# Gated FFN up projections as seven block products per weight tile pair

## The reference

```python
def swiglu(x, w_in, w_out):
    gate, up = jnp.split(x @ w_in, 2, axis=-1)
    return (jax.nn.silu(gate) * up) @ w_out

for l in range(DEPTH):       # DEPTH = 2, D_MODEL = 1024, D_FF = 2816, SEQ = 512, float32
    x = x + 0.5 * rms_norm(swiglu(rms_norm(x, ln_ffn1_pre[l]), w_ffn1_in[l], w_ffn1_out[l]), ln_ffn1_post[l])
    mix = token_mixing(rms_norm(x, ln_mix_pre[l]), ...)
    x = x + rms_norm(mix, ln_mix_post[l])
    x = x + 0.5 * rms_norm(swiglu(rms_norm(x, ln_ffn2_pre[l]), w_ffn2_in[l], w_ffn2_out[l]), ln_ffn2_post[l])
    gate = jax.nn.sigmoid(rms_norm(x, ln_ple_pre[l]) @ w_ple_gate[l])
    x = x + rms_norm(gate * (p[l] @ w_ple_proj[l]), ln_ple_post[l])
```

## Time and profile before

| | |
|---|---|
| time, median of 3 runs | 2898.39 us (2896.41 to 2900.55) |
| span of the profiled execution | 2896.7 us |
| PE busy | 2846.7 us, 98% |
| PE weight loads busy | 2402.4 us, 83% |
| DVE busy | 1379.2 us, 48% |
| ACT busy | 1141.2 us, 39% |
| POOL busy | 15.7 us, 1% |
| granted TensorE clock, mean | 0.997 |
| 512-column matmuls of L214 | 6048, mean 390 ns each from start to end |
| 256-column matmuls of L214 | 1536, mean 286 ns |

### The profile page before, as it was taken

The page is one execution under the profiler, slowest core; times in us unless marked ns, Lnnn a source line. Parts: engine busy times, 40 slices in busy tenths (PEclk is TensorE's granted clock), DMA queues, the critical chain, the costliest instruction groups (busy, mean ns, idle before and its releaser), DMA issues. The chain is left out here.

```text
span 2896.7 us, 41108 instructions
## 1 busy us (share of the span) xinstructions
PE 2846.7 (98%) x17248; PEld 2402.4 (83%) x17248; DVE 1379.2 (48%) x1923; ACT 1141.2 (39%) x1655; POOL 15.7 (1%) x29
## 2 busy tenths in 40 slices
PE   8999999999999999999999999999999999999998
PEld 7888888878888888888888877888888888888887
DVE  3334355676333355333336667333346258756541
ACT  3223244554232245222235555223236357544430
POOL 0000000000000000000000000000000000000000
PEclk9999999999999999999999999999999999999999
DMA  4233412103223431223412103122332111222331
GB/s 152 96 101 126 142 39 66 39 3 117 87 95 109 138 117 52 92 97 107 149 49 79 53 4 110 61 100 95 132 122 95 59 49 33 102 73 96 101 124 51
DMA packets 71415, 254.32 MB, mean 88 GB/s; under 512 B 8056, under 2 KB 9080, under 8 KB 71232
## 3 DMA queue, kind: packets, MB, share of 16 engines
q1 hardware_dynamic: 71232, 251.70, 25.9%
HBM read 249.57 MB, written 2.10 MB: 87 GB/s over the span
## 5 line engine op out<-in xcount | busy, mean ns | idle before, releaser
L214 PE MATMUL ps<-h_hi,w_space 128*128 128x512 f32 (+1 forms) x5056 | 1445.8, 370 | 3.0 <-DVE h_lo L312 3.0
L214 PEld LDWEIGHTS ps<-h_hi,w_space 128*128 128x128 f32 x5056 | 919.1, 189 | 163.8 <-DVE h_lo L312 3.8
L202 DVE TENSOR_TENSOR w_space<-w_raw,w_space 128x1024 fp32r<-128x1024 f32 x440 | 533.5, 1223 | 1015.7 <-ACT w_space L195 1015.6
L214 PE MATMUL ps<-h_lo,w_space 128*128 128x512 f32 (+1 forms) x2528 | 930.9, 368 | 0.0
L195 ACT CAST w_space<-w_raw 128x1024 fp32r<-128x1024 f32 x440 | 455.8, 1048 | 898.9 <-PE ps L214 551.1
L224 PE MATMUL ps<-w_space 128*128 128x512 f32 x3216 | 737.3, 390 | 1.3 <-PEq L91 0.8
L224 PEld LDWEIGHTS ps<-w_space 128*128 128x128 f32 x3216 | 602.0, 188 | 125.9 <-issue 1.2
L214 PEld LDWEIGHTS ps<-h_lo,w_space 128*128 128x128 f32 x2528 | 477.9, 189 | 77.5 <-issue 0.5
L607 ACT CAST w_space<-act_p 128x512 fp32r<-128x512 f32 x88 | 54.7, 621 | 186.1 <-DVE act_p L619 186.1
L622 DVE TENSOR_TENSOR w_space<-act_p,w_space 128x512 fp32r<-128x512 f32 x88 | 60.9, 692 | 60.5 <-ACT w_space L607 60.5
L619 DVE TENSOR_TENSOR act_p<-act_s,ps 128x512 f32<-128x512 f32 x88 | 59.9, 680 | 54.9 <-PE ps L214 54.9
(11 more groups left out here) (412 smaller groups left out, 2195.5 us busy)
## 6 DMA issues: line engine op xcount, KB each, us to landing
w_raw<-in_w_ffn_in SPq DMA_DIRECT2D x176, 512.0 KB, 3.4
w_raw<-in_w_ffn_out SPq DMA_DIRECT2D x88, 512.0 KB, 3.5
w_raw<-in_w_in SPq DMA_DIRECT2D x64, 512.0 KB, 3.4
w_raw<-in_w_up SPq DMA_DIRECT2D x44, 512.0 KB, 3.4
w_raw<-in_w_out SPq DMA_DIRECT2D x24, 512.0 KB, 4.0
w_raw<-in_w_down SPq DMA_DIRECT2D x22, 512.0 KB, 3.5
w_raw<-in_w_ple_gate SPq DMA_DIRECT2D x16, 512.0 KB, 3.5
gain_pre<-in_gains_pre SPq DMA_DIRECT2D x10, 512.0 KB, 4.8
```

The lines of the kernel that those rows point to most:

```text
L202: nc.vector.tensor_tensor(self.lo(n), self.raw[:, n % SLOTS, :], self.hi(n).bitcast(F32), ALU.subtract).then_inc(self.lo_ready, 1)
L214: m = nc.tensor.matmul(c.ps[:, bank, t], part[:, cols], moving[:, k, t], start=(k == 0 and i == 0), stop=(k == KD - 1 and i == 2))
```

## The change

A gate tile G and an up tile U over the halves of the contraction are the 2 x 2 blocks a11, a12 (of G) and a21, a22 (of U). h over the same halves and over the two halves of the tokens is b11, b12, b21, b22. The four blocks of the result are made from seven products instead of eight (Winograd's form), for pairs 3 to 21. Pairs 0 to 2 (`PLAIN = 3`) stay as they were.

The sums are s1 = a21 + a22, s2 = s1 - a11 ("early sums", `sums_early`), s3 = a11 - a21, s4 = a12 - s2 ("late sums"), t1 = b12 - b11, t2 = b22 - t1, t3 = b22 - b12, t4 = b21 - t2. s are made for every pair on DVE, t once an FFN; POOL first adds h_hi and h_lo again to whole values. Each operand of a product is split in hi and lo. The partial results are added in PSUM: ACT copies between halves of banks ("seeded"), and to SBUF ("kept", "carried"), and DVE adds them back ("c", "d").

```diff
-            ffn1.append(Ffn(c, turn, a["w_ffn1_in"][l], a["w_ffn1_out"][l], AFTER_PLE if l else FRESH, **after_ple))
+            ffn1.append(SevenFfn(c, turn, a["w_ffn1_in"][l], a["w_ffn1_out"][l], AFTER_PLE if l else FRESH, SPARE, **after_ple))
...
+    def tensor_product(self, pe, nc, q, name):
+        c = self.c
+        x_name, t_name, half = {"m1": ("a11", "b11", 0), "m5": ("s1", "t1", 1), "m6": ("s2", "t2", 0), "m2": ("a12", "b21", 0),
+                                "m7": ("s3", "t3", 0), "m3": ("s4", "b22", 1), "m4": ("a22", "t4", 0)}[name]
...
+        for k in range(HALF_K):
+            cols = slice(k * P, (k + 1) * P)
+            for i, (part, moving) in enumerate(((x_hi, t_hi), (x_hi, t_lo), (x_lo, t_hi))):
+                m = nc.tensor.matmul(out, part[:, cols], moving[:, k, :], start=(name == "m1" and k == 0 and i == 0),
+                                     stop=(k == HALF_K - 1 and i == 2), skip_group_check=(name != "m1"))
+        m.then_inc(c.seven_done, 1)
```

PE's order of the products, with what each waits for:

```diff
+        for q in range(PLAIN, KF):
+            if q > PLAIN:
+                pe.wait_ge(c.silu_ready, self.f0 + q - 3)
+            self.wait_rested(pe, "x", q, 0)
+            self.tensor_product(pe, nc, q, "m1")
+            self.wait_rested(pe, "x", q, 1)
+            self.tensor_product(pe, nc, q, "m5")
+            if q > PLAIN:
+                self.wait_rested(pe, "x", q - 1, 3)
+                self.wait_rested(pe, "d", q - 1)
+                self.tensor_product(pe, nc, q - 1, "m4")
+            self.wait_split(pe, "seeded", q)
+            self.tensor_product(pe, nc, q, "m6")
+            self.wait_split(pe, "kept", q)
+            self.tensor_product(pe, nc, q, "m2")
+            self.wait_split(pe, "carried", q)
+            self.wait_rested(pe, "x", q, 2)
+            self.tensor_product(pe, nc, q, "m7")
+            self.wait_rested(pe, "c", q)
+            self.tensor_product(pe, nc, q, "m3")
```

Operand part 0 is the gate unit (a11, a12), 1 the early sums, 2 the late sums, 3 the half unit a22. ACT's loop; t3's conversion and the wait for its lo stand ahead of it:

```diff
+        self.silu(act, nc, 2)
+        act.wait_ge(W.done, self.u0 + 2 * PLAIN)
+        self.t_hi(act, nc, "t3")
+        self.wait_rested(act, "t3")
+        for q in range(PLAIN, KF):
+            bank, other = self.bank(2 * q), self.bank(2 * q + 1)
+            if q > PLAIN:
+                self.silu(act, nc, q - 1)
+            self.part_hi(act, nc, q, 2)
+            if q < LAST:
+                self.part_hi(act, nc, q + 1, 0)
...
+            act.wait_ge(c.seven_done, self.done_no(q, "m5"))
+            if q > PLAIN:
+                act.wait_ge(c.product, self.f0 + q - 3)
+            nc.scalar.copy(c.ps[:, other, 0:HALF_T], c.ps[:, bank, 0:HALF_T]).then_inc(c.seven_split, 1)
+            if q >= PLAIN + 2:
+                self.wait_rested(act, "d", q - 2)
+            nc.scalar.copy(c.p[:, 0, (q % 2) * HALF_T:(q % 2 + 1) * HALF_T], c.ps[:, bank, HALF_T:S]).then_inc(c.seven_split, 1)
+            self.part_hi(act, nc, q, 3)
+            if q < LAST:
+                self.part_hi(act, nc, q + 1, 1)
...
+            act.wait_ge(c.seven_done, self.done_no(q, "m6"))
+            if q > PLAIN:
+                self.wait_rested(act, "c", q - 1)
+            nc.scalar.copy(c.p[:, 1, 0:HALF_T], c.ps[:, other, 0:HALF_T]).then_inc(c.seven_split, 1)
```

The acts are no longer split when they are made. They stay whole in the slots (`cells`), and each is split in the down phase into one of four places:

```diff
+    def act_hi(self, act, nc, k):
+        c = self.c
+        act.wait_ge(c.product, self.f0 + k + 1)
+        if k < 4:
+            act.wait_ge(c.seven_done, self.done_no(LAST, ("m5", "m6")[k // 2]))
+        else:
+            act.wait_ge(c.W.done, self.down.d0 + k - 3)
+        nc.scalar.copy(self.act_parts(k)[0], self.cell(k)).then_inc(c.act_hi, 1)
...
+    def scalar_down(self, act, nc):
+        for k in range(4, KF):
+            self.act_hi(act, nc, k)
+            self.c.W.hi_to(act, nc, self.down.d0 + k + 1)
```

`vector_down` does the same with the lo parts. The rows of w_out go through five slots in turn (`ROW_SLOTS`), so row k's conversion waits for row k-5. In the blocks these calls stand ahead of the conversions for the next phase, and SP loads all rows before it loads gains and masks (the masks still wait for `act_ready` of all 22 acts):

```diff
-                c.W.load_to(sp, ffn.down.d0 + SLOTS)
+                c.W.load_to(sp, ffn.down.d0 + KF)
+                ffn.wait_extra(sp)
                 proj.turn.load(sp)
                 attention.load(sp, ffn)
                 c.W.load_to(sp, proj.u0 + 12)
...
                 ffn.scalar(act, nc)
-                c.W.hi_to(act, nc, ffn.down.d0 + SLOTS)
                 start.scalar_tables(act, nc)
+                ffn.scalar_down(act, nc)
                 c.W.hi_to(act, nc, ffn.end() + EARLY)
                 turn_scalar(act, nc, proj.turn, ffn.down)
```

More of the change, by code:

```diff
@@ L153, with __init__ @@
 class Unit:
-    def __init__(self, n, slot, after, src):
-        self.n, self.slot, self.after, self.src = n, slot, after, src
+    def __init__(self, n, slot, after, load):
+        self.n, self.slot, self.after, self.load = n, slot, after, load
+class Load:
+    def __init__(self, src, freed):
+        self.src, self.freed = src, freed
 class Weights:
     def __init__(self, c, raw, sem):
-        self.c, self.raw, self.units, self.held = c, raw, [], {}
+        self.c, self.raw, self.units, self.loads, self.held = c, raw, [], [], {}
         self.raw_ready = [sem(f"w_raw_ready{s}") for s in range(SLOTS)]
@@ L170, in add, with add_raw @@
         n = len(self.units)
-        self.units.append(Unit(n, slot, self.held.get(slot), src))
-        self.held[slot] = n
-        return n
+        self.units.append(Unit(n, slot, self.held.get(slot), len(self.loads)))
+        self.loads.append(Load(src, (self.lo_ready, n + 1)))
+        self.held[slot] = (self.done, n + 1)
+        return n
+    def add_raw(self, src, freed):
+        self.loads.append(Load(src, freed))
+        return len(self.loads) - 1
     def hi(self, n):
@@ L179, in lo, with raw_of, wait_loaded @@
         return self.c.space[:, self.units[n].slot, 1, :]
+    def raw_of(self, i):
+        return self.raw[:, i % SLOTS, :]
+    def wait_loaded(self, eng, i):
+        eng.wait_ge(self.raw_ready[i % SLOTS], 16 * (i // SLOTS + 1))
     def load_to(self, sp, end):
[L182 to L186, removed]
+        last = self.units[end - 1].load + 1
+        while self.loaded < last:
+            i = self.loaded
+            if i >= SLOTS:
+                freed, count = self.loads[i - SLOTS].freed
+                sp.wait_ge(freed, count)
+            sp.dma_start(self.raw_of(i), self.loads[i].src).then_inc(self.raw_ready[i % SLOTS], 16)
             self.loaded += 1
@@ L191, in hi_to @@
             n = self.split
[L192 to L195, removed]
+            unit = self.units[n]
+            self.wait_loaded(act, unit.load)
+            if unit.after is not None:
+                freed, count = unit.after
+                act.wait_ge(freed, count)
+            nc.scalar.copy(self.hi(n), self.raw_of(unit.load)).then_inc(self.hi_ready, 1)
             self.split += 1
@@ L213, in products_up @@
         for i, (part, moving) in enumerate(((W.hi(n), c.h_hi), (W.hi(n), c.h_lo), (W.lo(n), c.h_hi))):
-            m = nc.tensor.matmul(c.ps[:, bank, t], part[:, cols], moving[:, k, t], start=(k == 0 and i == 0),
-                                 stop=(k == KD - 1 and i == 2))
+            m = nc.tensor.matmul(c.ps[:, bank, t], part[:, cols], moving[:, k, t], start=(opens and k == 0 and i == 0),
+                                 stop=(k == KD - 1 and i == 2), skip_group_check=not opens)
     return m
@@ L543, in wait_free @@
         if self.free[k] is not None:
-            eng.wait_ge(self.c.W.done, self.free[k] + 1)
+            freed, count = self.free[k]
+            eng.wait_ge(freed, count)
     def release(self, d0):
         for k in range(KF):
-            self.c.W.held[k // 2] = d0 + k
+            self.c.W.held[k // 2] = (self.c.W.done, d0 + k + 1)
 class Ffn(Up):
@@ L825, in __init__ @@
         for k in range(KD):
-            c.W.held[OPERANDS_AT + k // 2] = self.down.d0 + k
+            c.W.held[OPERANDS_AT + k // 2] = (c.W.done, self.down.d0 + k + 1)
     def place(self, w_out):
         self.early = EARLY_ROWS
-        self.c.W.held[MIX_OUT_SLOTS[4]] = len(self.c.W.units)
+        self.c.W.held[MIX_OUT_SLOTS[4]] = (self.c.W.done, len(self.c.W.units) + 1)
         self.down = Down(self.c, [w_out[k] for k in range(KD)], MIX_OUT_SLOTS)
```

349 lines of the change are left out of this document (337 added, 12 removed).

## The result

| | before | after |
|---|---|---|
| time, median | 2899.58 us (2896.41 to 2904.49) | 2903.26 us (2898.53 to 2910.01) |
| ratio to before, 95% interval | | 1.0013 [1.0007, 1.0019] |
| span of the profiled execution | 2896.7 us | 2900.6 us |
| granted TensorE clock, mean | 0.997 | 0.989 |

A forecast was written before the change was run, and what follows sets the result against it. The prediction took TensorE (PE), busy 2846.7 of 2896.7 us, as the bound. Its terms, -65.4 (products) + 8 (first pairs) + 36 (tails) + 6.4 (clock) = -15 us, gave 2883.4 us, range 2843 to 2912.

The forecast's parts named there:

- the tails: Ends of four FFNs: splitting acts there delays the norm before tile 0's transposes, 36 us together, bounds 10 to 46.
- Part 1, the rate: Pairs 3 to 21: 256-column matmuls start every 119.3 ns, saving 0.86 us a pair, 65.4 us over 76 pairs.
- Part 2, the walk: Seven-product loop: ACT and DVE keep up with PE, smallest slack 0.7 us, so it costs nothing.
- POOL additions ... hidden: Before the first changed pair: POOL's additions end 20 us before the products, so they cost nothing.
- The first changed pair: ACT's conversions ahead of "seeded" make m6 wait: 2.0 us, 8 us in four FFNs, bounds 0 to 12.
- Part 3, projection tails: FFN ends before projection: ACT's order and weights behind window masks stall tile 0's transposes 11.4 us, 11.1 more, twice.
- Part 3, PLE tails: FFN ends before PLE: act 21, row 21 and seven units precede the norm; stall 7.3 us, 7.0 more, twice.
- The clock: Behind the four tail stalls: PE runs at half rate for a while, 1.6 us each, 6.4 us, at least 0.
- A: Rival: tails are hidden and only the first changed pairs lose, -57 us, 2841 us; chance 0.22.
- B: Rival: ACT and DVE pace the seven-product loop, PE stopping 1 us a pair, +76, 2959 us; chance 0.11.
- C: Rival: waits at seven product boundaries a pair break up weight loads, 53 us, kernel at 2936; chance 0.05.

The follow-up runs named there:

- e9: The changed kernel with both late sums made twice in each of the 76 pairs, adding DVE work: 2902.93 us, ratio 1.0010.
- e1: The changed kernel with all four POOL additions waiting until h is whole: 2898.68 us, ratio 0.9994.
- e2: The changed kernel with copies seeded and kept ahead of the late-sum and next-gate conversions in the first changed pair: 2898.88 us, ratio 0.9998.
- e3: The changed kernel with SP loading the first three projection units ahead of the window masks: 2894.86 us, ratio 0.9983.
- e8: The kernel before the change, with ten useless ACT copies of 1024 columns ahead of the norm in the four tails: 2941.11 us, ratio 1.0141.
- e4: e3, with ACT and DVE converting only two next-phase units ahead of the norm, the others between its steps: 2862.68 us, ratio 0.9867.
- e7: The changed kernel with 34 zero-weight filler matmuls of 512 columns ahead of tile 0's transposes in the tails: 2899.99 us, ratio 0.9999.
- e10: The changed kernel with e1, e2 and e4, carried and add c earlier in first changed pairs, one lo earlier in PLE tails: 2849.65 us, ratio 0.9827.

## Why the prediction was wrong

Most mechanisms were read rightly, and the sum was not: -65 and +50 are terms that nearly cancel. The sum came out 18.7 us too low. The rate is 5.9 of it (4.6 by starts alone), the tails 4.4, the half clock behind them 3.2, the half clock behind small gaps 3.1 and POOL's additions 3.7; the last two stood at nothing. All five err in one direction.

- **Part 1, the rate,** is the largest term that was mis-sized. 119.3 ns was read over 15 starts of the earlier trace rows, where one hundredth of a microsecond in the printed starts is 0.7 ns a matmul. It is 120.0, and over 6384 matmuls that is 4.5 us. The saving was 59.5 to 60.8 us, below even the lower bound of 63.5. Both stretches that the prediction used are of some 20 matmuls. The trace of before has longer ones, here 143 in one of the up phases (timeline of PE, first and last):

```profile
708.68 0.28 PE L214 MATMUL ps<-h_lo,w_space 128*128 128x256 f32 x1
...
725.72 0.52 PE L214 MATMUL ps<-h_hi,w_space 128*128 128x256 f32 x2
```

  That is 17.04 us for 142 steps, 120.0 ns each. The rate could have been had before the change.
- **Part 2, the walk** held: no idle time in a steady pair, and the copies and adds shown above within 0.15 us of their places. e9 shows it by experiment: DVE had over 1 us to give.
- **"POOL additions ... hidden"** is the step that failed outright. They were placed 20 us ahead of their reader, which is true, but their cost is not lateness. They stretch DVE's operations beside them, at the start and in the first PLE, where DVE is what PE waits for: 3.7 us by the intervals, and by e1's ratio 5.5, with the half clock behind the start's gap. Their own duration was right: 2.6 us in e1 (2 x 1.29), 2.9 after.
- **The first changed pair**: 1.83 us of idle time four times, 2.08 by starts, for 2.0. Right, and e2 shows why taking two conversions out of the way gives nothing by itself: the next products wait for what was put behind.
- **Part 3, projection tails.** Nearly to the tenth: units at T + 5.7, 8.2 ... 14.0 (walked: 5.8, 8.5 ... 14.1), norm at T + 16.4 (16.6), stall 11.36 and 11.97 (11.4). e3 shows the masks to be 3.5 to 4 us of it. The rest is ACT's order together with raw places that come free late; e8 shows that lateness of ACT alone makes such stalls, and e4 that they go when the order is changed (with e3's loads).
- **Part 3, PLE tails**: 9.38 and 9.01 for 7.3. Here T is 1034.33. Units 0 to 3 came as walked (unit 3 at T + 6.2, walked 6.4), units 4 to 6 did not: started at T + 8.7, 10.7 and 12.0, where the walk had their ends at 8.7, 9.8 and 10.9. The timeline of ACT shows them waiting for their loads, and that of DVE when the raw places come free:

```profile
1042.99 1.05 ACT L223 CAST w_space<-w_raw 128x1024 fp32r<-128x1024 f32 x1 [1.39 <-DMA w_raw<-in_w_ple_gate]
1045.05 1.05 ACT L223 CAST w_space<-w_raw 128x1024 fp32r<-128x1024 f32 x1 [1.00 <-DMA w_raw<-in_w_ple_gate]
1046.33 1.04 ACT L223 CAST w_space<-w_raw 128x1024 fp32r<-128x1024 f32 x1 [0.23 <-DMA w_raw<-in_w_ple_gate]
```

```profile
1035.93 4.63 DVE L230 TENSOR_TENSOR w_space<-w_raw,w_space 128x1024 fp32r<-128x1024 f32 x4 [0.26 <-ACT w_space L223]
```

  DVE makes the lo of row 21 and of units 0 to 2 in one stretch, so unit 0's raw place is free at about 1038.2 (T + 3.9) and unit 4 lands 4.8 us later, at 1042.99, not the lone load's 3.4. The loads of units 3 to 6 are asked for 1.1 us apart and are in flight together. The DMA engines' busy share is 0.79 to 1.09 in each us from 1039 to 1047, so that they share the bandwidth is the likely reason; it wasn't tried by itself.
- **The clock**: 9.6 us behind the four stalls for 6.4, which was taken from one stretch at the start. e7 removes it in the two tails where the stall is filled nearly to its end. Two gaps of 1.8 us (before the transposes at 26.65 and in one first pair, 745.90) brought 1.5 us each as well, which the sum did not have at all.
- **Rivals.** A (tails hidden) did not happen in this kernel. Reordering gets near its time, 2841: e10, 2850. B (ACT and DVE set the pace) is refuted by the trace and by e9. C (boundaries of products) is refuted by the row of 36: the same 120.0 ns through three products as inside one.

What stays open: which of the gaps of 1.8 to 2 us is followed by the half clock. Three of the four first-pair gaps after were not, nor was the gap at the start in e2 and e3, 1.96 us there; in e2 it followed the gap of 1.93 in the first PLE instead. So the 3.1 us of the ledger belong to one profiled execution; those of e1, e2, e3, e7 and e9 had one such stretch or two in their FFNs. Without this term and POOL's, the rate, the tails and the clock behind them still turn the forecast gain of 15 us into one of 1.5.

## What to carry to other kernels

A saving on the bounding engine is real only as far as what follows the changed phase is still on time; here 60 us were saved and 50 given back at four places, 40 as idle time of PE and 10 as the slower clock behind it, where the norm's engine was given more jobs at the worst moment. So walk the end of a phase as carefully as its loop, and ask of each in-order engine what it has queued ahead of the next critical chain: reordering that queue, with three loads moved ahead (e4), was worth 43 us of span. When a forecast is a small difference of large terms, read rates over the longest stretch there is, and widen the middle case by the sum of the terms' errors.

## What the runs showed of the hardware

- Additions on POOL of 1024 columns from two SBUF inputs stretch a DVE operation beside them from 1.28 to 3.10 us or from 1.23 to 2.89; POOL's own mean goes from 2622 to 2923 ns. Work on an idle engine is not free for its neighbour.
- A stall of PE of 8 to 12 us cost 1.3 to 2.7 us more behind it in these runs, since PE then ran at 1.2 GHz for a while (PEclk 0.50). With filler matmuls that left 1.6 and 1.8 us idle this cost was gone; with 3.7 and 5.1 us left it was not. A gap of 1.8 us without filler was followed by it (1.5 us) in some cases and not in others.
- fp32r matmuls of 256 columns start every 120.0 ns, those of 512 every 226.7: seven products in place of eight save 7.4% of a pair's time, not 12.5%.
- ACT copies 256 columns from PSUM to PSUM in 0.36 us; PSUM to SBUF takes 0.36 to 0.38.
